# Weighting the fetched expert rows with a diagonal matrix on TensorE instead of scaling them on ScalarE and transposing

## The chip, the cores and the metric

One core of a Trainium2 chip runs the whole program. The metric is the device time of one execution in microseconds (us), the median of several runs. A profile is one more execution, taken by the hardware profiler.

## The reference

Two blocks of a language model on 256 tokens of width 1024, all in 32-bit floats. What matters here is the last part of each of the two layers of the second block, a feed-forward made of single experts. Each token picks 128 experts (8 heads x 16) of a table of 16384, by scores:

```python
expert = jnp.take_along_axis(cand_i, best_j, axis=-1)
gate = jax.nn.softmax(best_s, axis=-1)
act = jax.nn.gelu(jnp.einsum('btd,bthkd->bthk', xi, u_tab[expert]), approximate=False)
return jnp.einsum('bthk,bthkd->btd', (gate * act), v_tab[expert])
...
x = _layer_norm(DN_ALPHA * x + mix, ln1_g, ln1_b)
x = _layer_norm(DN_ALPHA * x + peer_ffn(x, peer_wq, peer_keys, peer_u, peer_v), ln2_g, ln2_b)
```

Every token needs 128 rows u (1024 wide) and 128 rows v (1024 wide) of its own; the result is the sum of the v rows, each times one number of that token and expert.

## The kernel before

The 256 tokens of a layer are two tiles of 128, so the second block has four tiles in order, i = 0 to 3 (layer i // 2, tokens i % 2). A tile has 128 **expert steps**, n = 128 i + k for k = 0 to 127, 512 in all. One step handles, for each of the 128 tokens (one for each partition), that token's k-th expert:

1. GpSimd (`fetch`, L2164 to L2171) issues an indirect DMA that brings 128 rows of 2048 floats (u and v side by side, 1.05 MB) from the table `in_puv` into `GR[n % PING]`. PING is 6, so the fetch of step n waits until TensorE is through with step n - 6 (`EP[n - PING]`).
2. VectorE (L2186) multiplies the u half by the token's row x and sums it into one number per partition.
3. ScalarE takes the Gelu of it (L2155), multiplies it by the gate (L2157) and then scales the v half, 1024 wide, by this number (L2160).
4. TensorE (L2141 to L2144) adds the scaled v half to PSUM banks 6 and 7 by eight transposes of 128 x 128, which accumulate over the 128 steps. So the sum stands there transposed.

When a tile's 128 steps are done, its closing part `fin` follows: VectorE (L2199) and ScalarE (L2263) copy banks 6 and 7 to the tile `YT`, TensorE transposes them back (`turn`, a helper at L435), VectorE adds them to x (L2205) and normalizes (L2209 to L2225), with one power on GpSimd (L2238). The first step of the next tile waits on TensorE until x has been added (`PV[i - 1, "x1"]`), since both use banks 6 and 7.

Between the expert steps of tile i stands the other work of tile i + 1 (the **lane**): projections (`fm` L1350, `tm` L1398), attention branches (`nsa` L1756 to L1785, `core` L1461 to L1509), gates (L1712), mixing (`mix`: L1888 and L1904), the `query` (L2017) and `route` (L2038 on TensorE, then sorting on VectorE) that pick the experts. The order is one written list, `plan`: every entry ("e", n) is one expert step, every entry (s, i) is one step of stream s of tile i. Each engine walks through the same list and issues its own part of each entry, in order; VectorE is at step n when ScalarE is at n - 1 and TensorE at n - 2. The lane of tile i + 1 is spread over the 128 entries by weights; the last tile has no lane but the closing part and its own routing. SyncE loads the weights of the lane in pieces of 1 MB into a ring of five slots, each load waiting until the slot's last reader on TensorE is through; these loads and the fetches share the same DMA engines.

Of the kernel before, what the change touches and what calls it, by code (L numbers as in the profile page):

```python
# [78 lines left out]
def build(nc, A, out):  # L79
# [4 lines left out]
    with ctx:  # L84
# [131 lines left out]
        SW2 = at(place(928), 928)  # L216
        scr = place(5554)
        GR = [at(place(2048), 2048) for i in range(PING)]
        YT = at(place(1024), 8, 128)
        IX = [at(place(128), 128).bitcast(u32) for t in range(2)]  # L220
        GT_ = [at(place(128), 128) for t in range(2)]
        DO = [at(place(128), 128) for t in range(2)]
# [39 lines left out]
                 + weave([("route", 20, 1), ("gates", 20, 1)])]  # L262
        for i in RI:
            placed_at = [(128.0 * i + k, ("e", 128 * i + k)) for k in range(128)]
            placed_at += [(128.0 * i + 1.1 + 0.1 * k, ("fin", i - 1)) for k in range(4) if i >= 1]
            lane = [("fin", i - 1)] * 8 * (i >= 1) + [(s, i + 1) for s in (tile_steps(i + 1) if i < 3 else [])]
            total, done = sum(weight[s] for s, _ in lane), 0.0
            for s in lane:
                placed_at.append((128.0 * i + 1.5 + 118 * done / total if i < 3 else 128.0 * i + 1.5 + done, s))
                done += weight[s[0]]  # L270
            lane = []
            for c in R3:
                lane += [("query", i)] * 8 + [("route", i)] * 20
            for n, s in enumerate(lane):
                placed_at.append((128.0 * i + 0.2 + 33.0 * n / len(lane), s))
            plan += [s for _, s in sorted(placed_at, key=lambda x: x[0])]
        plan += [("e", NE), ("e", NE + 1)] + [("fin", 3)] * 12


        RING2, SLOT2 = 5, 2048  # L280
# [2 lines left out]
                    tm=[("t", 0, 0, 3)] + [("t", n, 2 * n + 2, (7, 7, 11, 11, 13)[n - 1]) for n in range(1, 6)],  # L283
                    nsa=[("cw", 0, 0, 1)], gates=[("g", n, 2 * n, 4 * (n // 2) + 3) for n in range(16)],
                    mix=[("b", n, 2 * n + 2, 2 * n + 3) for n in R4] + [("o", n, 12 + n, 12 + (n | 1)) for n in R4] + [("ga", 0, 19, 21)],
                    query=[("q", n, 4 * n, 8 * (n // 2) + 7) for n in R8], fin=[("gf", 0, 8, 9)])
        step, nth2, last2 = {}, {}, {}
        for at_, s in enumerate(plan):
            n = step[s] = step.get(s, -1) + 1
# [115 lines left out]
        TA = marks("t_a", [(i, c, x) for i in RI for c in R4 for x in ("s", "e")])  # L405
        TV = marks("t_v", [(i, c, x) for i in RI for c in R4 for x in ("ix", "g3", "gt")])
        EP, EA, EV = [marks(n, range(NE)) for n in ("e_p", "e_a", "e_v")]
        PP = marks("p_p", [x for i in RI for x in [(i, "y0"), (i, "y1")] + [(i, c) for c in R2 if i < 2]])
        PV = marks("p_v", [(i, x) for i in RI for x in ["y", "x0", "x1", "st", "l"] + ["h"] * (i < 2)])
        PA = marks("p_a", [x for i in RI for x in [(i, "y")] + [(i, "h")] * (i < 2)])  # L410
        PO = marks("p_o", RI)


# [920 lines left out]
        def fm_pe(pe, i):  # L1334
            t = i % 2
            if i < 2:
                pe.wait_ge(*KV[t, 0])
                pe.wait_ge(*KA[t, 4])
            else:
                pe.wait_ge(*PV[i - 2, "h"])  # L1340
                pe.wait_ge(*PA[i - 2, "h"])
            for n in range(7):
                W = slot2(("f", i, n), 8, 256)
                pe.wait_ge(*landed2("f", i, n))
                if n in (4, 6):
                    pe.wait_ge(*MA[i, ("f", n // 2 - 2)])
                for h in R2:
                    o = bank(n // 2 % 2)[:, (n % 2 * 2 + h) * 128:(n % 2 * 2 + h) * 128 + 128]
                    for k in R8:
                        m = pe.matmul(o, W[:, k, h * 128:h * 128 + 128], HT[:, k, tsl(t)], start=k == 0, stop=k == 7)  # L1350
                        if k == 7 and h == 1 and (n % 2 == 1 or n == 6):
                            m.then_inc(MP.next((i, ("f", n // 2))), 1)
                        if k % 4 == 3:
                            yield
# [778 lines left out]
        def expert_pe(pe):  # L2133
            yield
            yield
            for n in range(NE):
                i, k = n // 128, n % 128
                if k == 0 and i:
                    pe.wait_ge(*PV[i - 1, "x1"])
                pe.wait_ge(*EA[n])  # L2140
                for c in R8:  # L2141
                    m = pe.matmul(bank(6 + c // 4)[:, tsl(c % 4)], GR[n % PING][:, 1024 + c * 128:1152 + c * 128], ident, is_transpose=True,  # L2142
                                  start=k == 0 and c % 4 == 0, stop=k == 127, skip_group_check=True)
                m.then_inc(EP.next(n), 1)  # L2144
                yield

        def expert_ac(ac):
            yield
            for n in range(NE):
                i, k = n // 128, n % 128  # L2150
                co, g = CO[i % 2][:, k:k + 1], GT_[i % 2][:, k:k + 1]
                if k % 32 == 0:
                    ac.wait_ge(*TV[i, k // 32, "gt"])
                ac.wait_ge(*EV[n])
                ac.activation(co, DO[i % 2][:, k:k + 1], ACT.Gelu).then_inc(oa.up(), 1)  # L2155
                ac.wait_ge(*oa.now())
                ac.activation(co, co, ACT.Copy, scale=g).then_inc(oa.up(), 1)  # L2157
                ac.wait_ge(*oa.now())
                v = GR[n % PING][:, 1024:2048]
                ac.activation(v, v, ACT.Copy, scale=co).then_inc(EA.next(n), 1)  # L2160
                yield
            yield

# [29 lines left out]
        def fin_ve(ve, i):  # L2193
            t = i % 2
            gb = slot2(("gf", i, 0), 2048)
            st, mv, v = ln_parts(t)
            x = X[:, t, :]
            ve.wait_ge(*EP[128 * i + 127])
            ve.tensor_copy(YT[:, 0:4, :], by(bank(6), 128)).then_inc(PV.next((i, "y")), 1)  # L2199
            yield  # L2200
            yield
            for h in R2:
                xx = x[:, h * 512:h * 512 + 512]
                ve.wait_ge(*PP[i, f"y{h}"])
                ve.scalar_tensor_tensor(xx, xx, al, bank(6 + h), MUL, ADD).then_inc(PV.next((i, f"x{h}")), 1)  # L2205
                yield
            ve.wait_ge(*PV[i, "x1"])
            for k in R2:
                ve.bn_stats(st[:, k * 6:k * 6 + 6], x[:, k * 512:k * 512 + 512]).then_inc(ov.up(), 1)  # L2209
            yield  # L2210
            ve.wait_ge(*ov.now())
            ve.bn_aggr(mv, by(st, 6)).then_inc(ov.up(), 1)
            yield
            ve.wait_ge(*ov.now())
            ve.tensor_scalar(v, v, 1.0, 1e-5, MUL, ADD).then_inc(PV.next((i, "st")), 1)
            yield
            ve.wait_ge(*PO[i])
            ve.tensor_scalar(x, x, mv[:, 0:1], v, SUB, MUL).then_inc(ov.up(), 1)
            yield
            ve.wait_ge(*landed2("gf", i, 0))  # L2220
            ve.wait_ge(*ov.now())
            ve.tensor_tensor(x, x, gb[:, 0:1024], MUL).then_inc(ov.up(), 1)
            yield
            ve.wait_ge(*ov.now())
            ve.tensor_tensor(x, x, gb[:, 1024:2048], ADD).then_inc(PV.next((i, "l")), 1)  # L2225
            yield
            yield
            if i < 2:
                ve.wait_ge(*PP[i, 0])
                ve.tensor_copy(HT[:, 0:4, tsl(t)], by(bank(0), 128)).then_inc(PV.next((i, "h")), 1)  # L2230
            yield

        def fin_po(po, i):
            v = ln_parts(i % 2)[2]
            for _ in R6:
                yield
            po.wait_ge(*PV[i, "st"])
            po.tensor_tensor(v, v, halfc, ALU.pow).then_inc(PO.next(i), 1)  # L2238
            for _ in R6:
                yield  # L2240

        def fin_pe(pe, i):
            yield
            for c in R2:
                pe.wait_ge(*(PV[i, "y"] if c == 0 else PA[i, "y"]))
                for k in R4:
                    m = turn(pe, bank(6 + c)[:, tsl(k)], YT[:, 4 * c + k, :])
                m.then_inc(PP.next((i, f"y{c}")), 1)
            yield
            for _ in R8:  # L2250
                yield
            if i < 2:
                pe.wait_ge(*PV[i, "l"])
                for c in R2:
                    for k in R4:
                        m = turn(pe, bank(c)[:, tsl(k)], X[:, i % 2, tsl(4 * c + k)])
                    m.then_inc(PP.next((i, c)), 1)
            yield
            yield

        def fin_ac(ac, i):
            ac.wait_ge(*EP[128 * i + 127])
            ac.activation(YT[:, 4:8, :], by(bank(7), 128), ACT.Copy).then_inc(PA.next((i, "y")), 1)  # L2263
            for _ in range(11):
                yield
            if i < 2:
                ac.wait_ge(*PP[i, 1])
                ac.activation(HT[:, 4:8, tsl(i % 2)], by(bank(1), 128), ACT.Copy).then_inc(PA.next((i, "h")), 1)
            yield


# [270 lines left out]
```

## Time and profile before

| | |
|---|---|
| time, median of 3 runs | 2911.42 us (2909.92 to 2918.89) |
| the profiled execution's own time | 2918.89 us |
| its span, first to last instruction | 2917.1 us |
| mean granted clock of TensorE | 0.869 of full speed |
| busy: TensorE, weight loads, VectorE, ScalarE, GpSimd | 81%, 69%, 48%, 45%, 25% of the span |
| expert steps: from the first transposes to the last | 1190 us to 2905 us |

"Granted clock" is the share of TensorE's full clock (2.4 GHz) that the chip let through, averaged over a stretch; at any moment it is one of two levels, 1.2 or 2.4 GHz. The DMA share is the mean busy share of the core's 16 DMA engines; it can read 1.01 by rounding. The expert steps fall into four **stages**, one for each tile, whose ends are the copies at L2199: at 1633, 2092, 2560 and 2905 us. A 32-bit matmul that is no transpose shows as two records, each with a weight load of its own; a transpose shows as one.

### The profile page before, as it was taken

The page shows a single profiled execution, that of the slowest core. Times are in us where ns is not written, and L with a number is a line of the kernel's source. Part 1 is how long each engine was busy: PE and PEld are TensorE (multiplying, and loading weights), DVE is VectorE, ACT ScalarE, POOL GpSimd, SP SyncE. Part 2 cuts the span into 40 slices and gives each one's busy share as a digit, 9 for nine tenths or more (in the row PEclk, how much of TensorE's full clock was granted, in tenths as well). Part 3 has the DMA queues.
Part 4 walks back from the last instruction along what each step waited for, and adds up shares of the span by engine and source line. Part 5 has one row for each costly group of instructions (what it writes and reads, how often), then busy time and mean ns, then how long its engine had stood idle before and what let it go on. Part 6 is the DMA issues. An engine that isn't in the chain of part 4 may idle for free.

```text
span 2917.1 us, 34012 instructions
## 1 busy us (share of the span) xinstructions
PE 2371.4 (81%) x13488; PEld 2003.1 (69%) x13488; DVE 1390.1 (48%) x3171; ACT 1310.5 (45%) x2339; POOL 737.8 (25%) x615
## 2 busy tenths in 40 slices
PE   7987998969999999878786788687698878666676
PEld 6766887856884878867665777566587766565554
DVE  3564333341001133474656764545765644676444
ACT  1551112110000220466755667764557674556665
POOL 0010112110000000232334323333322423334564
PEclk9988999989999999987777898899797988776666
DMA  6221111123433577998889999999998999999997
GB/s 257 87 89 58 59 65 58 51 101 126 163 144 139 218 271 288 395 420 347 306 348 422 403 421 383 409 408 415 396 420 355 407 366 420 401 380 351 421 421 318
DMA packets 109999, 839.34 MB, mean 288 GB/s; under 512 B 12176, under 2 KB 12432, under 8 KB 13968
## 3 DMA queue, kind: packets, MB, share of 16 engines
q0 software_dynamic: 73728, 536.90, 45.6%
q1 hardware_dynamic: 36112, 300.25, 26.2%
q8 instruction: 107, 1.75, 0.2%
q14 instruction: 52, 0.43, 0.0%
HBM read 836.06 MB, written 1.05 MB: 287 GB/s over the span
## 4 chain that ended last, share of the span: by engine, by line
PE 50%; DMA 20%; DVE 13%; ACT 12%; issue 3%; POOL 1%; SPq 0%; DVEq 0%; POOLq 0%; ACTq 0%
DMA mem<-in_puv,mem 19%; PE psm L431 10%; PE psm L2142 7%; PE psm L439 5%; PE psm L1712 5%; DVE mem L2186 4%; ACT mem L2160 4%; PE psm L718 3%; PE psm L2017 3%; PE psm L1247 3%; PE psm L1350 2%; PE psm L1904 2%; ACT L2155 1%; PE psm L733 1%; PE psm L435 1%
## 5 line engine op out<-in xcount | busy, mean ns | idle before, releaser
L2142 PE MATMUL psm<-mem 128*128 128x128 f32 x4096 | 706.6, 331 | 365.3 <-ACT mem L2160 364.7
L2142 PEld LDWEIGHTS psm<-mem 128*128 128x128 f32 x4096 | 587.4, 172 | 480.4 <-ACT mem L2160 464.8
L2170 POOL DMA_INDIRECT mem<-in_puv,mem x512 | 618.0, 1207 | 1111.0 <-PE psm L2142 1036.0
L2186 DVE CUSTOM_DVE_ANT_0 mem<-mem 128x1024 f32<-128x1024 f32 x512 | 624.5, 1225 | 436.2 <-DMA mem<-in_puv,mem 435.4
L2160 ACT ACTIVATE mem<-mem 128x1024 f32<-128x1024 f32 x512 | 588.8, 1150 | 16.7
L431 PE MATMUL psm<-mem 128*128 128x256 f32 (+2 forms) x1504 | 352.6, 398 | 32.6 <-DVE mem L1180 17.1
L431 PEld LDWEIGHTS psm<-mem 128*128 128x128 f32 x1504 | 293.2, 198 | 91.3 <-issue 29.5
L2155 ACT ACTIVATE mem<-mem 128x1 f32<-128x1 f32 x512 | 101.8, 199 | 457.2 <-DVE mem L2186 456.3
L1712 PE MATMUL psm<-mem 128*128 128x256 f32 x1024 | 245.4, 392 | 0.5 <-ACT mem L1426 0.5
L1712 PEld LDWEIGHTS psm<-mem 128*128 128x128 f32 x1024 | 195.9, 197 | 27.7 <-ACT mem L1426 0.9
L439 PEld LDWEIGHTS psm<-mem 128*128 128x128 f32 x1408 | 178.7, 192 | 45.2 <-issue 22.0
L439 PE MATMUL psm<-mem 128*128 128x128 f32 x1408 | 190.3, 279 | 19.4 <-ACT mem L986 5.9
L2157 ACT ACTIVATE mem<-mem 128x1 f32<-128x1 f32 x512 | 150.8, 294 | 16.6
L718 PE MATMUL psm<-mem 128*128 128x256 f32 x576 | 150.1, 384 | 0.0
L2017 PE MATMUL psm<-mem 128*128 128x128 f32 x1024 | 133.3, 286 | 6.3 <-DMA mem<-in_pwq 5.6
L2017 PEld LDWEIGHTS psm<-mem 128*128 128x128 f32 x1024 | 127.7, 202 | 8.6 <-DMA mem<-in_pwq 6.4
L986 ACT ACTIVATE mem<-psm 128x512 f32<-128x512 f32 x64 | 38.2, 597 | 209.8 <-PE psm L439 151.0
L1350 PE MATMUL psm<-mem 128*128 128x128 f32 x896 | 113.1, 279 | 7.9 <-DVE mem L2230 4.6
L435 PE MATMUL psm<-mem 128*128 128x128 f32 (+1 forms) x352 | 63.5, 319 | 62.4 <-DVE mem L1002 20.8
L1350 PEld LDWEIGHTS psm<-mem 128*128 128x128 f32 x896 | 107.2, 195 | 9.4 <-DVE mem L2230 5.2
L718 PEld LDWEIGHTS psm<-mem 128*128 128x128 f32 x576 | 100.3, 193 | 11.6 <-issue 3.9
L435 PEld LDWEIGHTS psm<-mem 128*128 128x128 f32 (+1 forms) x352 | 47.8, 162 | 76.3 <-DVE mem L1002 21.2
(357 smaller groups left out, 2435.5 us busy)
## 6 DMA issues: line engine op xcount, KB each, us to landing
mem<-in_w2g SPq DMA_DIRECT2D x64, 1024.0 KB, 8.9
mem<-in_w SPq DMA_DIRECT2D x18, 2048.0 KB, 8.3
mem<-in_pwq SPq DMA_DIRECT2D x32, 1024.0 KB, 11.5
mem<-in_w2f SPq DMA_DIRECT2D x28, 1024.0 KB, 10.1
mem<-in_wgu SPq DMA_DIRECT2D x11, 2048.0 KB, 7.9
mem<-in_w2t SPq DMA_DIRECT2D x20, 1024.0 KB, 11.9
mem<-in_w2b SPq DMA_DIRECT2D x16, 1024.0 KB, 10.7
mem<-in_w2o SPq DMA_DIRECT2D x16, 1024.0 KB, 9.6
```

What stands on the lines that cost most here:

```text
L431: m = pe.matmul(o, lhs(k), rhs(k), start=start and k == ks[0], stop=stop and k == ks[-1])
L435: return pe.transpose(o, i, ident[0:i.shape[0], 0:i.shape[0]])
L439: m = pe.matmul(b[:, u * 128:u * 128 + 128], lhs(u), rhs(u), start=True, stop=True)
L718: m = pe.matmul(o, W[:, k, c0:c0 + 128], HT[:, k, :], start=k == 0, stop=k == 7)
L1350: m = pe.matmul(o, W[:, k, h * 128:h * 128 + 128], HT[:, k, tsl(t)], start=k == 0, stop=k == 7)
L1712: m = pe.matmul(gates_bank(i, n // 2)[:, n % 2 * 256:n % 2 * 256 + 256], HT[:, k, tsl(t)], W[:, k, :], start=k == 0, stop=k == 7)
L2017: m = pe.matmul(o, W[:, k, h * 128:h * 128 + 128], HT[:, k, tsl(t)], start=k == 0, stop=k == 7)
L2142: m = pe.matmul(bank(6 + c // 4)[:, tsl(c % 4)], GR[n % PING][:, 1024 + c * 128:1152 + c * 128], ident, is_transpose=True, start=k == 0 an ...
L2157: ac.activation(co, co, ACT.Copy, scale=g).then_inc(oa.up(), 1)
L2160: ac.activation(v, v, ACT.Copy, scale=co).then_inc(EA.next(n), 1)
L2170: po.indirect_dma_start(GR[n % PING], None, A[f"puv{i // 2}"], bass.IndirectOffsetOnAxis(ap=IX[i % 2][:, k:k + 1], axis=0)).then_inc(gsem[ ...
L2186: ve.tensor_tensor_reduce(out=GR[n % PING][:, 0:1024], in0=GR[n % PING][:, 0:1024], in1=X[:, i % 2, :], scale=1.0, scalar=0.0, op0=MUL, op ...
```

## The change

ScalarE no longer scales the v half. It writes a 128 x 128 matrix with the token's number on the diagonal (the identity `ident` scaled per partition by `co`) into one of four buffers `DG`, and waits before it for the step that used the buffer four steps earlier. TensorE then multiplies this diagonal, as the stationary operand, with the v half as it was fetched, in two matmuls of 512 columns, accumulated in banks 6 and 7. The sum then stands in PSUM as tokens x features, so the two copies to `YT`, the eight transposes back and their waits go, and VectorE adds banks 6 and 7 to x at once. The first four steps of `fin`, which stood at 1.1 to 1.4 entries after the stage's start, and the eight others become ten in the lane, from 1.5 entries on; the steps after the addition move up by two. `YT` (1024 floats per partition) gives way to `DG` (512).

```diff
-        YT = at(place(1024), 8, 128)
+        DG = at(place(512), 4, 128)
...
-            placed_at += [(128.0 * i + 1.1 + 0.1 * k, ("fin", i - 1)) for k in range(4) if i >= 1]
-            lane = [("fin", i - 1)] * 8 * (i >= 1) + [(s, i + 1) for s in (tile_steps(i + 1) if i < 3 else [])]
+            lane = [("fin", i - 1)] * 10 * (i >= 1) + [(s, i + 1) for s in (tile_steps(i + 1) if i < 3 else [])]
...
-        plan += [("e", NE), ("e", NE + 1)] + [("fin", 3)] * 12
+        plan += [("e", NE), ("e", NE + 1)] + [("fin", 3)] * 10
...
-                for c in R8:
-                    m = pe.matmul(bank(6 + c // 4)[:, tsl(c % 4)], GR[n % PING][:, 1024 + c * 128:1152 + c * 128], ident, is_transpose=True,
-                                  start=k == 0 and c % 4 == 0, stop=k == 127, skip_group_check=True)
+                for h in R2:
+                    m = pe.matmul(bank(6 + h), DG[:, n % 4, :], GR[n % PING][:, 1024 + h * 512:1536 + h * 512], start=k == 0, stop=k == 127)
                 m.then_inc(EP.next(n), 1)
...
-                v = GR[n % PING][:, 1024:2048]
-                ac.activation(v, v, ACT.Copy, scale=co).then_inc(EA.next(n), 1)
+                if n >= 4:
+                    ac.wait_ge(*EP[n - 4])
+                ac.activation(DG[:, n % 4, :], ident, ACT.Copy, scale=co).then_inc(EA.next(n), 1)
...
             ve.wait_ge(*EP[128 * i + 127])
-            ve.tensor_copy(YT[:, 0:4, :], by(bank(6), 128)).then_inc(PV.next((i, "y")), 1)
-            yield
-            yield
             for h in R2:
                 xx = x[:, h * 512:h * 512 + 512]
-                ve.wait_ge(*PP[i, f"y{h}"])
                 ve.scalar_tensor_tensor(xx, xx, al, bank(6 + h), MUL, ADD).then_inc(PV.next((i, f"x{h}")), 1)
...
-            yield
-            for c in R2:
-                pe.wait_ge(*(PV[i, "y"] if c == 0 else PA[i, "y"]))
-                for k in R4:
-                    m = turn(pe, bank(6 + c)[:, tsl(k)], YT[:, 4 * c + k, :])
-                m.then_inc(PP.next((i, f"y{c}")), 1)
-            yield
...
-            ac.wait_ge(*EP[128 * i + 127])
-            ac.activation(YT[:, 4:8, :], by(bank(7), 128), ACT.Copy).then_inc(PA.next((i, "y")), 1)
-            for _ in range(11):
+            for _ in range(9):
```

## Rows read from the trace of the kernel before

**Rows 1.** The page, costliest groups: busy us, mean ns of one, idle before.

```profile
L2142 PE MATMUL psm<-mem 128*128 128x128 f32 x4096 | 706.6, 331 | 365.3 <-ACT mem L2160 364.7
...
L2160 ACT ACTIVATE mem<-mem 128x1024 f32<-128x1024 f32 x512 | 588.8, 1150 | 16.7
...
L2157 ACT ACTIVATE mem<-mem 128x1 f32<-128x1 f32 x512 | 150.8, 294 | 16.6
```

**Rows 2.** Windows by stage: length, busy PE PEld DVE ACT POOL, clock, DMA, GB/s.

```profile
1190.00:1633.00 443.00, 334.85 (x2059) 294.17 (x2059) 261.58 (x651) 277.94 (x487) 153.70 (x133) 0.79 0.94 372
1633.00:2092.00 459.00, 351.60 (x2287) 304.76 (x2285) 263.30 (x662) 283.08 (x500) 155.19 (x135) 0.88 0.99 405
2092.00:2560.00 468.00, 372.41 (x2358) 324.13 (x2356) 271.52 (x665) 284.29 (x500) 157.17 (x135) 0.86 0.97 396
2560.00:2905.00 345.00, 239.95 (x1227) 198.85 (x1225) 202.93 (x459) 219.63 (x397) 171.90 (x124) 0.66 0.96 389
```

**Rows 3.** Windows of the transposes L2142 alone, the same stages (PE, PEld, clock, DMA).

```profile
1190.00:1633.00 443.00, 174.10 (x1019) 146.71 (x1020) 0.79 0.94 372
1633.00:2092.00 459.00, 155.76 (x1031) 130.54 (x1029) 0.88 0.99 405
2092.00:2560.00 468.00, 160.19 (x1026) 135.78 (x1024) 0.86 0.97 396
2560.00:2905.00 345.00, 216.46 (x1027) 174.34 (x1025) 0.66 0.96 389
```

**Rows 4.** Timeline near 2747 us, last stage: two steps' transposes, a fetch between.

```profile
2746.37 1.83 PE L2142 MATMUL psm<-mem 128*128 128x128 f32 x8 [0.58 <-ACT mem L2160]
...
2748.47 1.82 POOL L2170 DMA_INDIRECT mem<-in_puv,mem  x1 [0.66 <-PE psm L2142]
...
2748.80 1.10 PE L2142 MATMUL psm<-mem 128*128 128x128 f32 x8 [0.60 <-ACT mem L2160]
```

**Rows 5.** Timeline of TensorE, back to back: transposes and 512-column matmuls in turn.

```profile
1483.65 1.88 PE L1888 MATMUL psm<-mem 128*128 128x512 f32 x4
1485.37 1.04 PE L2142 MATMUL psm<-mem 128*128 128x128 f32 x8
1486.25 1.88 PE L1888 MATMUL psm<-mem 128*128 128x512 f32 x4
```

**Rows 6.** The chain near 1994 us: a burst of 256-column matmuls after transposes alone.

```profile
1994.09 3.41 PE psm L1904 x8
...
1998.38 3.46 PE psm L1904 x16
```

**Rows 7.** Groups by form: ScalarE over 128 x 128 with one operand for each partition.

```profile
L1801 ACT ACTIVATE mem<-mem 128x128 f32<-128x128 f32 x16 | 6.3, 393 | 2.9 <-DVE mem L1843 2.9
```

**Rows 8.** Windows of three shorter stretches, columns as in rows 2.

```profile
1314.00:1533.00 219.00, 169.93 (x936) 144.10 (x937) 114.95 (x239) 143.72 (x248) 74.27 (x64) 0.74 0.87 334
2117.00:2190.00 73.00, 66.91 (x547) 63.25 (x545) 45.57 (x139) 42.59 (x76) 20.85 (x20) 0.98 1.01 420
2190.00:2263.00 73.00, 61.81 (x390) 54.77 (x391) 41.06 (x117) 49.88 (x82) 19.59 (x18) 0.79 0.85 345
```

**Rows 9.** Windows of the transposes L2142 alone, the same stretches (PE, clock, DMA).

```profile
1314.00:1533.00 219.00, 84.54 (x480) 0.74 0.87 334
2117.00:2190.00 73.00, 20.86 (x152) 0.98 1.01 420
2190.00:2263.00 73.00, 22.26 (x144) 0.79 0.85 345
```

**Rows 10.** The chain, by line, within 1314 to 1533 us, then 2190 to 2263 us.

```profile
by line: DMA mem<-in_puv,mem 15.4%; PE psm L2142 14.8%; ACT mem L2160 10.0%; PE psm L1904 6.1%; ACT L2155 4.1%; DVE mem L2186 3.8%; PE psm L1758 3.2%; PE psm L1756 3.0%; ACT mem L2157 2.5%; issue 2.5%; PE psm L1888 2.4%; ACT mem L1801 2.0%;
...
by line: PE psm L2142 14.8%; ACT mem L2160 14.2%; PE psm L1712 9.6%; PE psm L1758 9.5%; ACT L2155 8.8%; ACT L1529 7.0%; PE psm L1398 6.2%; PE psm L1756 5.3%; PE psm L1469 4.5%; ACT mem L2157 3.8%; issue 3.0%; ACT mem L2155 2.0%; ACT mem L15
```

**Rows 11.** Timeline of the end: the last transposes, then the addition.

```profile
2903.12 1.96 PE L2142 MATMUL psm<-mem 128*128 128x128 f32 x8 [0.47 <-ACT mem L2160]
...
2906.56 1.28 DVE L2205 SCALAR_TENSOR_TENSOR mem<-mem,psm 128x512 f32<-128x512 f32 x2 [0.76 <-PE psm L435]
```

More of the change, by code:

```diff
@@ L285, in build @@
                     mix=[("b", n, 2 * n + 2, 2 * n + 3) for n in R4] + [("o", n, 12 + n, 12 + (n | 1)) for n in R4] + [("ga", 0, 19, 21)],
-                    query=[("q", n, 4 * n, 8 * (n // 2) + 7) for n in R8], fin=[("gf", 0, 8, 9)])
+                    query=[("q", n, 4 * n, 8 * (n // 2) + 7) for n in R8], fin=[("gf", 0, 6, 7)])
         step, nth2, last2 = {}, {}, {}
@@ L407, in build @@
         EP, EA, EV = [marks(n, range(NE)) for n in ("e_p", "e_a", "e_v")]
-        PP = marks("p_p", [x for i in RI for x in [(i, "y0"), (i, "y1")] + [(i, c) for c in R2 if i < 2]])
-        PV = marks("p_v", [(i, x) for i in RI for x in ["y", "x0", "x1", "st", "l"] + ["h"] * (i < 2)])
-        PA = marks("p_a", [x for i in RI for x in [(i, "y")] + [(i, "h")] * (i < 2)])
+        PP = marks("p_p", [(i, c) for i in R2 for c in R2])
+        PV = marks("p_v", [(i, x) for i in RI for x in ["x0", "x1", "st", "l"] + ["h"] * (i < 2)])
+        PA = marks("p_a", R2)
         PO = marks("p_o", RI)
@@ L1340, in fm_pe @@
                 pe.wait_ge(*PV[i - 2, "h"])
-                pe.wait_ge(*PA[i - 2, "h"])
+                pe.wait_ge(*PA[i - 2])
             for n in range(7):
@@ L2234, in fin_po @@
             v = ln_parts(i % 2)[2]
-            for _ in R6:
+            for _ in range(4):
                 yield
@@ L2267, in fin_ac @@
                 ac.wait_ge(*PP[i, 1])
-                ac.activation(HT[:, 4:8, tsl(i % 2)], by(bank(1), 128), ACT.Copy).then_inc(PA.next((i, "h")), 1)
+                ac.activation(HT[:, 4:8, tsl(i % 2)], by(bank(1), 128), ACT.Copy).then_inc(PA.next(i), 1)
             yield
```

## The prediction

> **What bounds the kernel now.** I read the windows by stage first. In the four stages of expert steps the DMA engines are busy 0.94, 0.99, 0.97 and 0.96 of the time [rows 2]. The reader is to see that no engine comes near that: TensorE 76, 77, 80 and 70%, ScalarE 63, 62, 61 and 64%. A stretch with a DMA share of 1.01 moves 420 GB/s [rows 8]; I take this as the ceiling. A fetch of 1.05 MB is then 2.5 us, and 128 of them 320 us, to which the lane's weights are added. All idle DMA time in the stages is 0.06 x 443 + 0.01 x 459 + 0.03 x 468 + 0.04 x 345 = 27 + 5 + 14 + 14 = 60 us. The change moves no byte, so what it can give is at most these 60 us and the end of the kernel.
>
> The same windows in shorter stretches show where the idle DMA time lies: 28 us from 1314 to 1533 us (share 0.87 of 219 us) and 11 us from 2190 to 2263 us (0.85 of 73 us) [rows 8]. These are the attention parts of the lane, where work goes back and forth between the engines. The chain says what the time goes by there: it passes through transposes, ScalarE's scaling and the table changes of the Gelu (L2155 without "mem"), with the fetches only 15% of the first stretch and none of the second's leading lines [rows 10].
>
> The page's groups give the price of the two operations to be replaced: 1150 ns for the scaling, and 706.6 us in all for 4096 transposes, 1.38 us for a step's eight [rows 1]. This is a mean over two clocks. In the timeline eight transposes last 1.10 us or 1.83 us within two and a half us of each other [rows 4], and the granted clock of the last stage, where TensorE does little else, is 0.66, that of the mixed stages 0.79 to 0.88 [rows 2].
>
> **The change part by part.**
>
> *ScalarE.* 512 times 1150 ns over 1024 columns becomes 128 columns. The nearest row is an activation of that shape with one operand for each partition, 393 ns [rows 7]. That saves 0.757 us a step, 97 us of ScalarE a stage, leaving it near 40% busy. The new wait for the step four earlier is priced at nothing: TensorE has ended step n - 4 two fetches after step n - 6, which lets fetch n begin, and fetch n has yet to arrive. If that cover fails, what waits behind it on ScalarE are its lane activations, and TensorE is late anyway then.
>
> *TensorE.* Eight transposes become two matmuls of 512 columns, four records. Between 1483.65 and 1486.25 us both kinds stand back to back at full clock: four records of 512 columns take 1.72 us, eight transposes 0.88 us [rows 5]. So a step costs 1.72 us at full clock, 0.84 us more than the transposes at full clock, and about as much as they do at the low one.
>
> What that makes of the clock decides the sum. After waiting with only transposes before it, a burst of eight records of 256 columns took 3.41 us (0.43 us each, the low clock); right after it sixteen took 3.46 us (0.22 us each, the high one) [rows 6]. Ordinary matmuls brought the clock up within one burst. The new step is such a burst in every 2.5 us, so I take the clock as full through all stages. The Trainium skill says in "TensorE: Matmul & The Clock Gate", Part 4, that transposes do not count towards the fast clock the way matmuls do; the 0.66 of the last stage, with TensorE 70% busy, agrees.
>
> TensorE's work by stage is then its other work at full clock plus 128 x 1.72 = 220 us. The other work is the difference of busy times times the granted clock [rows 2, 3]:
> - stage 0: (334.85 - 174.10) x 0.79 = 127; with 220, 347 us, 78% of 443
> - stage 1: (351.60 - 155.76) x 0.88 = 172; 392 us, 86% of 459 (77% before)
> - stage 2: (372.41 - 160.19) x 0.86 = 183; 403 us, 86% of 468 (80% before)
> - stage 3: (239.95 - 216.46) x 0.66 = 16; 236 us, 68% of 345.
>
> It stays below the DMA engines' time in each, though not in each stretch. From 2117 to 2190 us it was 66.91 us busy (92%) beside a full DMA [rows 8]; so 92% still leaves the DMA full. There it becomes (66.91 - 20.86) x 0.98 + 19 x 1.72 = 77.8 us in 73 [rows 8, 9]: 5 us longer. This is the front of a stage: `fm` beside `query` and `route`. Stage 1 has the same front, 5 us, and I give stage 0 half, 2 us. Loss: 12 us.
>
> *The slack stretches.* From 1314 to 1533 us the scaling is 10.0% of the chain, 21.9 us, and shrinks by 0.757 / 1.15: -14.4 us. Transposes are 14.8%, 32.4 us; a step's cost there 84.54 / 60 = 1.41 us [rows 9], so 23 steps pay 0.31 us more: +7.1 us. The small matmuls L1756 and L1758, 13.6 us of the chain, speed up from a clock of 0.74 to 1, about -3.5 us. Sum -10.8 us, of 28 to be had. From 2190 to 2263 us likewise: scaling 14.2%, 10.4 us, -6.8; transposes 10.8 us at 22.26 / 18 = 1.24 us a step, 8.7 steps, +4.2; other matmuls 35% of the chain, 25.6 us, at 0.79, -5.4. Sum -8.0 us, of 11. For the 20 us of idle DMA left elsewhere I take a quarter, -5 us, because much of it lies near sorting on VectorE, which stays.
>
> *The closing part.* The last transposes start at 2903.12 us and the addition at 2906.56 us, 3.44 us later [rows 11]. After, the last step starts 0.76 us earlier, its four records last 1.88 us from first start to last end [rows 5], and the addition follows at once: -2.3 us. In the three stages before, the copies and transposes go as well, but VectorE now does an expert step between the two halves of the addition, because its two steps stand half an entry apart. I set this against each other: nothing. On GpSimd the power waits for VectorE's variance with the fetches queued behind it; it moves up by the same two steps as that variance, so the wait keeps its length. The lane behind the closing part shifts by about one entry of 128, and its loads with it: nothing. If that cover is gone it costs one step of 2.5 us a stage.
>
> **The sum.** -10.8 - 8.0 - 5 - 2.3 + 12 = -14 us. Against the profiled execution's own 2918.9 us this is 2905 us. That execution was the slowest of the three, 7.5 us above the median, so I forecast 2897 us beside the median of 2911.4.
>
> Bounds: the diagonal lies between 294 ns, the price of one column [rows 1], and 1150 ns, that of 1024, but far nearer to the row of its own shape; at 294 ns the two chains above give 3 us more, at 1150 ns they give back the 21 us won on ScalarE. The slack can give 60 us at most, and nothing at least. The dense fronts can cost from nothing (buffers absorb it: six fetches and five weight slots) to 25 us.
>
> **The rivals.**
>
> *TensorE becomes the bound of the mixed stages.* 86% is an average the engine has not had here, since the lane's matmuls come in bursts and wait for other engines. It decides where TensorE can't be held above some share: at 82% busy, stage 1 takes 392 / 0.82 = 478 us (+19) and stage 2 403 / 0.82 = 491 us (+23). With -11 us from stage 0 and -2 us at the end this is +29 us, 2940 us. At 86% it costs nothing, at 80% +69 us less 13. For it: the 77 to 80% of before. Against it: 92% in one stretch with a full DMA, and that TensorE's largest wait in before, 364.7 us for the scaling [rows 1], is time that it can fill.
>
> *The DMA hides everything.* What the slack stretches give back, the dense fronts take, and only the end is left: -2 us, 2909 us. For it: shares of 0.96 and more in three stages.
>
> *More of the slack is used.* If ScalarE's 97 us a stage is what keeps fetches waiting all over, half of the 60 us comes back and the fronts cost little: about -35 us, 2876 us. Against it: the fetches are on most of the chain where the DMA is full, and there ScalarE's time buys nothing.
>
> *The clock stays low.* A step would cost 3.41 us, as the eight records of 256 columns did [rows 6], and the last stage 128 x 3.41 + 23 = 460 us in place of 345: 3025 us, more if the mixed stages follow. Against it: rows 6.
>
> *The matmul costs four transposes' time.* A step is then 4 x 0.88 = 3.5 us at full clock, over a fetch's 2.5: the stages become 572, 617, 628 and 461 us, 563 us more, 3475 us. That is what the Trainium skill would make of it, in "TensorE: Matmul & The Clock Gate", Terms: the transpose mode is four times as fast for 32-bit data. The rows show 1.72 against 0.88 us, a factor of 2.0, for the same 1024 columns.
>
> **How the numbers follow.** The exchange as summed, 2880 to 2914 us: 0.42. More of the slack, 2855 to 2880: 0.10. DMA hides everything: 0.15. TensorE the bound, 2920 to 2965: 0.28. Clock low 0.04, four times 0.01. A measurement here tells 0.3% from no change, 2902.7 to 2920.2 us. Of the first case about three quarters lies below that, all of the second; of the others, the third is inside and the rest above: faster 0.44, no change 0.25, slower 0.31. The range leaves out the low clock, the four times and the ends of two cases: 2865 to 2950 us.
>
> **What would show it.** In the profile after: L2142 as 2048 records of 512 columns, four in 1.72 us; L2160 near 0.39 us; a granted clock of 0.95 or more in all stages; no L2199, L2263; the addition right behind the last step. The stretch 1314 to 1533 us shorter with a fuller DMA, the fronts of stages 1 and 2 longer with TensorE above 92%. Wrong would be: stages 1 and 2 longer than 459 and 468 us with a DMA share below 0.93 and TensorE in full use, or a stage 3 unlike 345 us.

## The result and the profile after

The changed kernel takes 2941.78 us, median of 4 runs (2937.18 to 2946.53; three more executions took 2939.60, 2946.96 and 2948.82 us), against 2910.67 us for the kernel before (4 runs): a ratio of 1.0108, 95% interval 1.0085 to 1.0133. It is 31 us slower, where 2897 us was forecast. The profiled execution has a span of 2942.0 us and a mean granted clock of 0.959, against 0.869.

Lines have moved: L2142 is now L2141, L2160 is L2159, L2170 is L2169, L435 is L434. First the page of the changed kernel, its costliest groups:

```profile
L2141 PE MATMUL psm<-mem 128*128 128x512 f32 x2048 | 1017.6, 626 | 157.9 <-ACT mem L2159 153.2
...
L2159 ACT ACTIVATE mem<-mem 128x128 f32<-128x128 f32 x512 | 206.0, 402 | 16.9
```

Against [rows 1], ScalarE's 588.8 us are 206.0 us, as priced (402 ns against 393 ns). The steps' matmuls are busy 1017.6 us in place of 706.6 us, and TensorE's idle time before them, most of it waiting for ScalarE, fell from 365.3 to 157.9 us.

Then the windows of the four stages, all engines, and the step's matmuls alone (columns as in [rows 2, 3]; the stages end at the additions, at 1625, 2103, 2581 and 2932 us):

```profile
1190.00:1625.00 435.00, 390.72 (x1553) 227.84 (x1552) 261.67 (x652) 185.23 (x488) 148.47 (x133) 0.95 0.95 379
1625.00:2103.00 478.00, 435.35 (x1759) 271.25 (x1758) 262.52 (x661) 185.27 (x500) 153.59 (x135) 0.95 0.96 390
2103.00:2581.00 478.00, 443.92 (x1837) 280.07 (x1836) 270.18 (x664) 186.48 (x495) 149.69 (x135) 0.96 0.95 384
2581.00:2932.00 351.00, 277.87 (x705) 112.11 (x703) 202.74 (x459) 124.85 (x396) 127.90 (x124) 0.98 0.96 385
```

```profile
1625.00:2103.00 478.00, 252.18 (x512) 94.19 (x512) 0.95 0.96 390
2103.00:2581.00 478.00, 250.90 (x513) 94.24 (x512) 0.96 0.95 384
```

Stages 1 and 2 lasted 459 and 468 us, now 478 and 478. TensorE is busy 91 and 93% in them (77 and 80% before), the granted clock is 0.95 and more, and the DMA share fell from 0.99 and 0.97 to 0.96 and 0.95: no more bytes, but more time in which the DMA engines had nothing to move. ScalarE went from 62 to 39%.

TensorE's own waits in stages 1 and 2 say where the idle time went. Before, from 1633 to 2560 us (waiter, who was waited for, us in total, times, longest):

```profile
PE psm L2142 <- ACT mem L2160: 165.9, 96, 7.4
...
PE psm L435 <- DVE mem L2225: 5.1, 2, 2.6
```

and after, from 1625 to 2581 us:

```profile
PE psm L2141 <- ACT mem L2159: 46.5, 38, 5.0
PE psm L434 <- DVE mem L2220: 13.3, 2, 6.6
```

The wait for the step's input shrank by 119 us, and all of TensorE's idle time in the two stages by 126 us, from 203 to 77 us. Its busy time grew by 435.35 + 443.92 - 351.60 - 372.41 = 155 us. The difference, 29 us, is what the two stages got longer. This is bookkeeping and names no cause yet.

### The profile page after: what moved, and what is told of

The parts are those of the page before. It is cut to its first block, busy times and chain, and to the rows that moved or that the text cites. A ratio compares the mean times of both kernels' runs of the same rounds, so it can differ in the third digit from the quotient of the medians.

```text
span 2942.0 us, 30348 instructions
## 1 busy us (share of the span) xinstructions
PE 2618.3 (89%) x11408; PEld 1770.9 (60%) x11408; DVE 1387.1 (47%) x3167; ACT 925.3 (31%) x2331; POOL 679.5 (23%) x615
## 4 chain that ended last, share of the span: by engine, by line
PE 62%; DMA 15%; DVE 12%; ACT 8%; issue 2%; POOL 1%; SPq 0%; DVEq 0%; POOLq 0%; ACTq 0%
PE psm L2141 16%; DMA mem<-in_puv,mem 13%; PE psm L430 10%; PE psm L1711 6%; PE psm L438 5%; DVE mem L2185 3%; PE psm L717 3%; PE psm L2016 3%; PE psm L1349 3%; PE psm L1246 3%; PE psm L1903 2%; PE psm L1397 1%; DMA mem<-in_pwq 1%; PE psm L434 1%; PE psm L732 1%
## 5 line engine op out<-in xcount | busy, mean ns | idle before, releaser
L2141 PE MATMUL psm<-mem 128*128 128x512 f32 x2048 | 1017.6, 626 | 157.9 <-ACT mem L2159 153.2
L2169 POOL DMA_INDIRECT mem<-in_puv,mem x512 | 563.0, 1100 | 1209.6 <-PE psm L2141 1141.6
L2141 PEld LDWEIGHTS psm<-mem 128*128 128x128 f32 x2048 | 373.7, 196 | 609.1 <-ACT mem L2159 300.4
L430 PEld LDWEIGHTS psm<-mem 128*128 128x128 f32 x1504 | 291.2, 196 | 92.0 <-issue 32.1
L1711 PEld LDWEIGHTS psm<-mem 128*128 128x128 f32 x1024 | 197.2, 194 | 56.7 <-issue 31.4
L2159 ACT ACTIVATE mem<-mem 128x128 f32<-128x128 f32 x512 | 206.0, 402 | 16.9
L438 PE MATMUL psm<-mem 128*128 128x128 f32 x1408 | 190.3, 279 | 19.4 <-ACT mem L985 5.9
L438 PEld LDWEIGHTS psm<-mem 128*128 128x128 f32 x1408 | 178.7, 192 | 45.3 <-issue 22.0
L2016 PEld LDWEIGHTS psm<-mem 128*128 128x128 f32 x1024 | 125.8, 195 | 29.8 <-issue 22.2
L2016 PE MATMUL psm<-mem 128*128 128x128 f32 x1024 | 128.8, 279 | 5.8 <-DMA mem<-in_pwq 5.1
L1349 PEld LDWEIGHTS psm<-mem 128*128 128x128 f32 x896 | 108.5, 192 | 22.5 <-issue 21.3
L434 PE MATMUL psm<-mem 128*128 128x128 f32 (+1 forms) x320 | 53.9, 304 | 67.8 <-DVE mem L1001 20.8
L1349 PE MATMUL psm<-mem 128*128 128x128 f32 x896 | 110.3, 275 | 2.0 <-DMA mem<-in_w2f 1.2
L717 PEld LDWEIGHTS psm<-mem 128*128 128x128 f32 x576 | 100.1, 193 | 11.3 <-issue 3.6
L434 PEld LDWEIGHTS psm<-mem 128*128 128x128 f32 (+1 forms) x320 | 41.2, 154 | 97.6 <-issue 32.7
## 6 DMA issues: line engine op xcount, KB each, us to landing
mem<-in_pwq SPq DMA_DIRECT2D x32, 1024.0 KB, 10.8
```

The source lines that it names most:

```text
L430: m = pe.matmul(o, lhs(k), rhs(k), start=start and k == ks[0], stop=stop and k == ks[-1])
L434: return pe.transpose(o, i, ident[0:i.shape[0], 0:i.shape[0]])
L438: m = pe.matmul(b[:, u * 128:u * 128 + 128], lhs(u), rhs(u), start=True, stop=True)
L717: m = pe.matmul(o, W[:, k, c0:c0 + 128], HT[:, k, :], start=k == 0, stop=k == 7)
L1711: m = pe.matmul(gates_bank(i, n // 2)[:, n % 2 * 256:n % 2 * 256 + 256], HT[:, k, tsl(t)], W[:, k, :], start=k == 0, stop=k == 7)
L2141: m = pe.matmul(bank(6 + h), DG[:, n % 4, :], GR[n % PING][:, 1024 + h * 512:1536 + h * 512], start=k == 0, stop=k == 127)
```

## The experiments

The step numbers n let two profiles be laid on each other. The table has the time from VectorE's start on step a to that on step b, from the timeline's rows of its product (L2186 of the kernel before), in us. Each is one execution.

| kernel | 0 to 128 | 128 to 256 | 256 to 384 | 384 to 511 | 128 to 144 | 160 to 176 | 288 to 304 |
|---|---|---|---|---|---|---|---|
| before | 457.0 | 459.3 | 468.5 | 343.6 | 61.6 | 60.8 | 65.9 |
| before, again | 450.7 | 461.4 | 465.3 | 345.2 | 59.2 | 62.3 | 63.3 |
| changed | 449.5 | 477.5 | 479.2 | 349.4 | 73.2 | 68.3 | 71.8 |
| changed, again | 449.2 | 476.3 | 480.3 | 348.5 | 71.6 | 68.3 | 70.0 |
| scalar_only | 444.5 | 456.4 | 457.9 | 341.4 | 60.6 | 57.8 | 61.7 |
| tensor_only | 458.7 | 481.6 | 491.4 | 350.1 | 70.2 | 72.0 | 72.9 |
| half_columns | 451.3 | 456.0 | 459.6 | 343.4 | 62.6 | 62.7 | 64.4 |
| three_quarters | 444.8 | 465.3 | 470.6 | 346.3 | 67.4 | 64.4 | 66.2 |
| closing_early | 447.3 | 473.1 | 482.0 | 348.3 | 65.8 | 64.8 | 67.0 |
| front_thinned | 456.0 | 475.4 | 486.7 | 346.5 | 63.5 | 66.3 | 68.5 |

**Two more profiles: before_again, after_again.** Both kernels unchanged, one execution each. Expected:

> The kernel before once more, for a second profile. It says how far the start of a given expert step moves between two executions of one kernel; theory A's reading of the stages needs this to be within some 5 us at step 384, while a first profile that was slow by itself in stage 0 would take away the changed kernel's lead of 7.5 us at step 128.

> The changed kernel once more, for a second profile with the same aim. Theory A: steps 128 to 144 and 256 to 272 take 70 to 73 us again, against 60 to 62 us in the kernel before.

Measured: 2914.36 and 2942.84 us. The changed kernel repeats within 2 us in every column. The kernel before repeats within 3.2 us but for stage 0, where the first profile was 6 us slow. So most of the lead of 7.5 us that the changed kernel seemed to have at step 128 was that of one execution: against the second profile it is 3 us at step 128, 1.5 us over the stage. The losses in stages 1 and 2 (15 to 18 and 11 to 15 us) and in stage 3 (3 to 6 us) stand.

**ScalarE's part alone: scalar_only.**

```diff
-                v = GR[n % PING][:, 1024:2048]
+                v = GR[n % PING][:, 1024:1152]
```

> The kernel before, with ScalarE scaling only the first 128 of a v half's 1024 columns; the other 896 go into the sum unscaled. It has ScalarE's relief (1150 to about 400 ns a step) and nothing of TensorE's part. Theory A, TensorE's longer step is what costs the time and ScalarE's relief wins some: 10 to 25 us below the kernel before, about 2893 us. Theory B, the DMA hides ScalarE's relief altogether: 2911 us within 4.

Measured: 2891.21 us, ratio 0.9929 (0.9908 to 0.9949), 21 us faster. Its windows by stage (all engines):

```profile
1190.00:1618.00 428.00, 325.07 (x2049) 286.42 (x2049) 259.72 (x648) 183.83 (x484) 153.79 (x133) 0.80 0.96 383
1618.00:2075.00 457.00, 356.98 (x2284) 312.73 (x2283) 264.42 (x663) 189.23 (x500) 156.00 (x136) 0.87 0.99 408
2075.00:2532.00 457.00, 360.88 (x2361) 316.47 (x2360) 271.12 (x667) 191.74 (x500) 153.60 (x135) 0.88 0.98 403
```

With ScalarE as idle as in the changed kernel, TensorE is at 76 to 79% and the DMA share is 0.96 to 0.99. The relief reaches the end, a little in every stage.

**TensorE's part alone: tensor_only.**

```diff
-                    m = pe.matmul(bank(6 + h), DG[:, n % 4, :], GR[n % PING][:, 1024 + h * 512:1536 + h * 512], ...)
+                    m = pe.matmul(bank(6 + h), ident, GR[n % PING][:, 1024 + h * 512:1536 + h * 512], ...)
...
-                if n >= 4:
-                    ac.wait_ge(*EP[n - 4])
-                ac.activation(DG[:, n % 4, :], ident, ACT.Copy, scale=co).then_inc(EA.next(n), 1)
+                v = GR[n % PING][:, 1024:2048]
+                ac.activation(v, v, ACT.Copy, scale=co).then_inc(EA.next(n), 1)
```

> The changed kernel, with ScalarE scaling the whole v half as before and TensorE multiplying by the plain identity in two matmuls of 512 columns. It has TensorE's part and the new closing part, and nothing of ScalarE's relief. Theory A, TensorE's longer step costs and ScalarE's relief wins: above the changed kernel's 2942 us by what ScalarE wins, 2950 to 2970 us. Theory B, the diagonal's own wait for the step four earlier holds ScalarE up: no slower than the changed kernel, 2942 us or less, since that wait is gone.

Measured: 2978.4 us, ratio 1.0227 (1.0204 to 1.0249), 65 us slower and 8 us beyond what was expected. The four kernels make a square, each beside the kernel before:

| | transposes | two matmuls of 512 columns, new closing part |
|---|---|---|
| ScalarE scales 1024 columns | 1 | 1.0227 |
| ScalarE's short operation | 0.9929 | 1.0108 |

TensorE's part costs 2.3% by itself and 1.8% (1.0108 / 0.9929) beside the relief; the relief is worth 0.7% beside transposes and 1.2% (1.0108 / 1.0227) beside the matmuls. The wait for the step four earlier isn't the cause. The slower tensor_only, which lacks it, also lacks the relief and so can't tell alone; but in the page of the changed kernel ScalarE is idle before the diagonal for 16.9 us in all 512 steps, against 16.7 us before the scaling [rows 1].

**A dose of TensorE's time: half_columns and three_quarters.** The same step with 256 or 384 of 512 columns in each matmul.

```diff
-                for h in R2:
-                    m = pe.matmul(bank(6 + h), DG[:, n % 4, :], GR[n % PING][:, 1024 + h * 512:1536 + h * 512], start=k == 0, stop=k == 127)
+                w = 512 if k in (0, 127) else 256
+                for h in R2:
+                    m = pe.matmul(bank(6 + h)[:, 0:w], DG[:, n % 4, :], GR[n % PING][:, 1024 + h * 512:1024 + h * 512 + w], start=k == 0, stop=k == 127)
```

> The changed kernel, with each matmul of a step over 256 columns in place of 512, but for the first and last step of a tile; the second half of each bank lacks 126 of 128 steps. A step costs TensorE 0.86 us, as the transposes did at full clock; ScalarE, the closing part and the clock stay as changed. Theory A, TensorE's time is the cause: the whole loss goes and ScalarE's gain is left, 2875 to 2900 us. Theory C, the closing part or the order of the plan is the cause: 2930 us or more.

> The changed kernel, with each matmul of a step over 384 columns in place of 512, but for the first and last step of a tile; a quarter of each bank lacks 126 of 128 steps. A step costs TensorE 1.29 us at full clock. 256 columns gave 2896 us, 512 give 2942 us. Theory A, TensorE's time adds up along the stretches where TensorE is the bound: about halfway, 2912 to 2925 us. Theory D, the loss comes from the clock's rise or from reading 512 columns at once: near one of the two ends.

Measured: 2896.32 us with 256 columns, ratio 0.9940 (0.9918 to 0.9961); 2915.84 us with 384, ratio 1.0012 (0.9997 to 1.0026); 1.0108 with 512. Everything but the width is the changed kernel (part of the sum is left out), so its loss goes with TensorE's time. By the ratios the first step of 128 columns adds 21 us and the second 28 us, of 512 x 0.43 = 220 us at full clock each (an estimate: a step's four records, each 128 columns or 0.11 us longer): a tenth of it, then an eighth, reaches the end. One expectation was missed: the clock did not stay as changed. With half the columns it fell to 0.872 (0.945 with 384); so the first of these steps mixes width and clock.

**The closing part: closing_early.** The addition's two halves back at entries 1.1 and 1.2.

```diff
+            placed_at += [(128.0 * i + 1.1 + 0.1 * k, ("fin", i - 1)) for k in range(2) if i >= 1]
-            lane = [("fin", i - 1)] * 10 * (i >= 1) + ...
+            lane = [("fin", i - 1)] * 8 * (i >= 1) + ...
```

> The changed kernel, with the two halves of the closing addition put back ahead of the next tile's second expert step (entries 1.1 and 1.2), the other eight closing steps as in the kernel before. Theory A, TensorE's longer step is the cause: it wins back little, 2935 to 2942 us. Theory C, the closing part's new place is the cause, since TensorE waits 6.6 us for the normalized x at the front of stages 1 and 2, 2.6 us before: it wins back 10 us or more, 2932 us or less.

Measured: 2937.51 us, ratio 1.0087 (1.0065 to 1.0109), beside 1.0108 (1.0085 to 1.0133). The two intervals overlap. At the front of stage 1 the steps 128 to 144 do get shorter, 65.8 us against 73.2 and 71.6, and TensorE's wait for the normalized x, 13.3 us above, is 4.4 us in its trace:

```profile
PE psm L435 <- DVE mem L2221: 4.4, 2, 2.2
```

but most isn't kept to the end: stages 1 and 2 together (steps 128 to 384) take 955.1 us, against 956.7 and 956.6 us. By the medians it is 4 to 6 us of the 31, and the intervals don't tell it from nothing.

**The order of the plan: front_thinned.** The same kernel, with the lane less dense at a stage's front:

```diff
-                placed_at.append((128.0 * i + 1.5 + 118 * done / total if i < 3 else 128.0 * i + 1.5 + done, s))
+                placed_at.append((128.0 * i + 1.5 + 118 * (done / total) ** 0.85 if i < 3 else 128.0 * i + 1.5 + done, s))
```

> The kernel with the closing part early again (2937.5 us), and the lane's steps spread less densely at the front of a stage: the share of the lane done is raised to the power 0.85 to give its place among the entries. No work is changed. Theory A says that TensorE is the bound in the dense fronts and nearly everywhere in stages 1 and 2 (91% busy), so the front gets shorter and the rest longer: 2925 to 2940 us. If the density of the fronts alone is the cause, 2915 us or less.

Measured: 2955.1 us, ratio 1.0142 (1.0115 to 1.0169): slower than either expected. The front did get shorter (128 to 144 in 63.5 us) and the rest lost more: against closing_early, stage 0 is 9 us longer, stage 1 2 us and stage 2 5 us. That an even spread doesn't help agrees with a TensorE that is short of time nearly everywhere, but why it costs some 16 us (by the ratios) was not traced, and stage 0, the largest loss, is not one where the changed kernel loses.

**Where TensorE has room: tile_0 and tiles_0_3.** The kernel before, with the changed step for some tiles only (`DIAG = (0,)` or `(0, 3)`, `if i in DIAG` at each changed place).

> The kernel before, with the diagonal and the two matmuls for the steps of tile 0 alone; tiles 1 to 3 keep scaling and transposes. Up to step 128 the changed kernel was 7.5 us ahead, in the stage whose lane is lightest. Theory A: 4 to 10 us below the kernel before, about 2906 us, since TensorE is not the bound in stage 0. If the steps cost alike everywhere, a quarter of the loss: 2919 us.

> The kernel before, with the diagonal and the two matmuls for tiles 0 and 3, which have the lightest lanes, and the closing part of these two in its short form, early. Theory A: the gain of tile 0 and the 2 us of the shorter end, against some 4 us at the front of stage 3 with its query and route: 2900 to 2910 us.

Measured: 2910.8 us, ratio 0.9996 (0.9983 to 1.0009), and 2911.64 us, ratio 0.9994 (0.9981 to 1.0008). Neither gains or loses. Both expectations leaned on the first profile of the kernel before, slow in stage 0, and fell with it. In stage 0 of tile_0 (window of all engines) the step's price is paid and refunded. Its first 16 steps take 75.1 us (71.1 and 69.6 in the two profiles of the kernel before), its steps 36 to 96 212.9 us (224.0 and 216.8):

```profile
1190.00:1625.00 435.00, 388.61 (x1577) 228.74 (x1576) 263.41 (x656) 187.46 (x490) 149.76 (x135) 0.96 0.95 380
```

**The relief without TensorE's price: vector_half.** The kernel before, with VectorE scaling half of the columns one step behind its product:

```diff
-                v = GR[n % PING][:, 1024:2048]
+                v = GR[n % PING][:, 1024:1536]
...
+                if n:
+                    scale_half(ve, n - 1)
...
+        def scale_half(ve, n):
+            v = GR[n % PING][:, 1536:2048]
+            ve.wait_ge(*EA[n])
+            ve.tensor_scalar(v, v, CO[n // 128 % 2][:, n % 128:n % 128 + 1], None, MUL).then_inc(EW.next(n), 1)
```

> The kernel before, with the scaling of the v half shared: ScalarE scales 512 columns and VectorE, one step behind its own product, the other 512; transposes and closing part stay. ScalarE's relief without TensorE's longer step. With only 128 columns scaled on ScalarE, and nowhere else, the time was 2891 us. Theory A: ScalarE is on the path where the DMA is slack; 0.43 of the 0.75 us a step gives some 12 us, less what VectorE's added 0.45 us costs in the sorting stretches: 2898 to 2908 us. If VectorE's in-order wait for ScalarE holds its lane up: 2915 us or more.

Measured: 2967.29 us, ratio 1.0166 (1.0141 to 1.0192), as the other branch of the expectation had it, only more. VectorE's waits:

```profile
DVE mem L2198 <- ACT mem L2160: 151.0, 75, 15.1
```

VectorE, the engine that starts every step, now stands 151 us behind ScalarE, with its lane and its next product behind that wait. That this wait makes the loss is argued, not tested. No version tried beats the kernel before with its work whole.

## Why the prediction was wrong

**What held.** The step's price and form, back to back in the changed kernel at full clock (timeline of TensorE), 1.72 us a step as [rows 5] said:

```profile
2129.12 1.89 PE L2141 MATMUL psm<-mem 128*128 128x512 f32 x4
2130.84 1.95 PE L1349 MATMUL psm<-mem 128*128 128x128 f32 x16
2132.63 1.89 PE L2141 MATMUL psm<-mem 128*128 128x512 f32 x4
```

The factor of 2 against transposes held, so the rival with a factor of 4 fell, and so did the one of a low clock: 0.95 to 0.98 by stage, though full "through all stages", as forecast, it was not. The end, in the timeline of the changed kernel:

```profile
2929.49 1.99 PE L2141 MATMUL psm<-mem 128*128 128x512 f32 x4 [0.47 <-ACT mem L2159]
2931.51 1.28 DVE L2200 SCALAR_TENSOR_TENSOR mem<-mem,psm 128x512 f32<-128x512 f32 x2 [3.08 <-PE psm L2141]
```

From the last step's first record to the addition it is 2.02 us, and 3.44 us in [rows 11]; with the 0.75 us that ScalarE is faster, -2.2 us against -2.3 forecast.

**The step that failed** is what was drawn from the sentence that TensorE's work "stays below the DMA engines' time in each, though not in each stretch", with 86% of stages 1 and 2: that the DMA engines' time would cover it, but for 12 us in the dense fronts, and that the slack stretches would gain 10.8 and 8.0 us. The work measured, 435 and 444 us, is 95% of the 459 and 468 us before; it is still below the DMA engines' time, and it wasn't covered. Three things were wrong.

1. *The work was too small.* It had 392 and 403 us for stages 1 and 2; busy are 435 and 444 us. The step's matmuls are busy 252 and 251 us where 220 were counted. A step lasts 1.89 us from first start to last end also back to back (0.17 us of it beside the next records) and 1.99 us alone, as at 2929.49 above; and 8 steps of stage 1 and 7 of stage 2 met the low clock and took 2.3 to 3.8 us. The other work is 183 and 193 us where 172 and 183 were counted. Times the granted clock of 0.95 and 0.96 it is 174 and 185 us: this other work was counted right, and the clock that was taken as full is not full, above all at the small attention matmuls (last section).

2. *The fronts.* Forecast was 5 us each in stages 1 and 2. Steps 128 to 144 took 10 to 14 us more and with closing_early 4 to 7 us more. So the term was about right for TensorE's work, and the other half came from the closing part, costed at nothing. The timeline of the changed kernel at the front of stage 1 shows how:

```profile
1628.67 2.82 PE L2141 MATMUL psm<-mem 128*128 128x512 f32 x4 [2.06 <-DVE mem L2200]
...
1635.03 0.60 ACT L2027 ACTIVATE mem<-psm 128x512 f32<-128x512 f32 x1 [9.24 <-PE psm L2016]
...
1638.33 0.87 DVE L2059 MAX8 mem<-mem 128x8 f32<-128x128 f32 x4 [6.96 <-ACT mem L2048]
...
1640.26 0.81 DVE L2213 TENSOR_SCALAR mem<-mem 128x1024 f32<-128x1024 f32 x1
...
1647.84 1.97 PE L434 MATMUL psm<-mem 128*128 128x128 f32 x8 [6.64 <-DVE mem L2220]
```

TensorE first waits 2.06 us for the second half of the addition, which stands behind an expert step on VectorE. Its query matmuls (L2016) come later by that and partly at the low clock, ScalarE and VectorE wait for them (the sorting at L2059), and the normalization (L2213 to L2220) stands behind the sorting in VectorE's order. So TensorE waits 6.6 us for x in place of 2.6 us. In closing_early two of the normalization's three passes stand ahead of the sorting, and TensorE's wait is 2.2 us. As most of that is lost again later in the stage, the closing part explains half of the front's loss and little of the 31 us.

3. *The attention stretches.* This is the sign error. There the DMA had slack, and I took from it that ScalarE's relief would fill it, with TensorE's longer steps only on the part of the chain that they held. But in such a stretch of the kernel before (1754 to 1815 us, steps 160 to 176), TensorE's wait for ScalarE was short:

```profile
PE psm L2142 <- ACT mem L2160: 6.7, 4, 4.5
```

6.7 us in 61 us is all that a faster ScalarE could shorten or a longer TensorE could fill (scalar_only takes 3.0 to 4.5 us off these steps). After, the wait is 0.2 us and TensorE fills its windows (1760 to 1828 us, 2232 to 2303.5 us, all engines):

```profile
1760.00:1828.00 68.00, 65.17 (x294) 42.51 (x293) 27.78 (x73) 32.16 (x76) 19.95 (x18) 0.87 0.82 327
2232.00:2303.50 71.50, 67.28 (x309) 45.30 (x307) 29.78 (x74) 33.27 (x78) 19.56 (x18) 0.88 0.78 314
```

Busy 96 and 94%, with DMA shares of 0.82 and 0.78: so what the DMA lacked was fetches released by TensorE, and its slack grew: GpSimd's fetches wait 48 us for TensorE in the first of these windows, and 36 us in the stretch of the kernel before. These 16 steps take 6 to 8 us and 4 to 9 us longer, where 8 us less were forecast for the stretch of the second. The low clock adds to it: at 2279.94 us a step takes 3.73 us, and the eight transposes in its place took 1.97 us (last section), so there the exchange costs 1.8 us and not 0.84 us.

Of the gain of 10.8 us from 1314 to 1533 us a part came. Steps 36 to 96 took 224.0 us in the profile it was read from and 216.8 us in the second; in the changed kernel they take 212.1 and 213.9 us. That is 3 to 5 us against the second profile. The front of stage 0 took it back, priced at 2 us: steps 0 to 16 take 74.7 and 74.6 us, against 71.1 and 69.6 us. The stage as a whole gives 1 to 2 us (steps 0 to 128: 450.7 us before, 449.5 and 449.2 us after).

**The rival that came true** is "TensorE becomes the bound of the mixed stages": 2940 us, by stages of 478 and 491 us at 82%. Measured were 2941.8 us, 478 and 478 us; the forecast work over the measured length is 392 / 478 = 82% and 403 / 478 = 84%. It got the sum largely by luck. Its condition, that TensorE can't be held above 82%, did not hold: TensorE was busy 91 and 93%, and the 82% comes out only because the forecast work was too small by as much. It also took 11 us from stage 0, which gave 1 to 2 us, 23 us for stage 2, which lost 11 to 15, and nothing for stage 3, which lost 3 to 6. What is right in it is that TensorE became the bound. The argument used against it, that TensorE's largest wait "is time that it can fill", is what the runs settle. In stages 1 and 2 it filled 119 of 166 us, and the rest of the added work came on top. Half_columns and three_quarters show that TensorE's time makes the loss, and the square shows that ScalarE's relief is real and worth less. Why a tenth to an eighth of the added time reaches the end, and not more or less, is argued from the waits and was not measured on its own.

Two slips in the prediction's sums change nothing here. By its own cases, slower comes to 0.33 and faster to 0.42, where it has 0.31 and 0.44; and at 80% busy the two stages take 67 us more, where it has 69.

## What to carry to other kernels

When work moves from one engine to another, weigh what the receiving engine waits for in each stretch, not its busy share over a stage: the new work is free only up to that wait. A slack DMA beside an engine that hardly waits is a sign that this engine is the bound, also when the chain of waits names others. Take a second profile before a difference of some microseconds between two stretches carries an argument.

## What the hardware showed that was not expected

**Low clock with ordinary matmuls too.** The prediction laid the low clock of the last stage to transposes, with the Trainium skill's rule in "TensorE: Matmul & The Clock Gate", Part 4, that they don't count towards the fast clock as matmuls do. The runs don't show a difference of kind. In the last stage of half_columns, where each step is four records of ordinary matmuls, 200 us have a granted clock of 0.64, in the changed kernel 1.00, and in the kernel before 0.63 (half_columns: window and a step in the timeline; then the windows of the changed kernel and of the kernel before):

```profile
2700.00:2900.00 200.00, 140.45 (x303) 79.47 (x301) 98.07 (x159) 67.45 (x225) 68.89 (x71) 0.64 0.93 385
...
2799.55 2.07 PE L2142 MATMUL psm<-mem 128*128 128x256 f32 x4 [0.41 <-ACT mem L2160]
```

```profile
2700.00:2900.00 200.00, 159.42 (x324) 55.03 (x323) 96.34 (x157) 70.50 (x235) 80.13 (x82) 1.00 1.01 420
...
2700.00:2900.00 200.00, 141.10 (x640) 113.26 (x640) 98.82 (x160) 131.61 (x241) 115.93 (x77) 0.63 1.00 417
```

The 640 records before are all transposes, so a mean of 0.63 says that with transposes alone the full clock was granted for about a quarter of the time. half_columns and the changed kernel differ in the columns of a step alone. The kind of matmul doesn't explain the low clock here.

**The clock falls under the small attention matmuls.** In `nsa` TensorE works through 64 records over 64 partitions with 15 columns each, then 64 with 64 columns each (with 7 for 15 in stage 1), without a gap between them. In the kernel before (timeline, then windows of the two bursts):

```profile
2239.01 3.93 PE L1756 MATMUL psm<-mem 64*64 64x15 f32 x64
2242.87 7.00 PE L1758 MATMUL psm<-mem 64*15 64x64 f32 x64
2249.80 1.97 PE L2142 MATMUL psm<-mem 128*128 128x128 f32 x8
...
2239.00:2242.87 3.87, 3.87 (x65) 3.83 (x65) 1.23 (x2) 2.86 (x5) 0.95 (x1) 0.98 1.00 417
2242.87:2249.87 7.00, 7.00 (x66) 6.80 (x66) 0.00 (x0) 0.13 (x1) 0.00 (x0) 0.50 0.81 338
```

and in the changed kernel:

```profile
2265.03 4.58 PE L1755 MATMUL psm<-mem 64*64 64x15 f32 x64
2269.54 7.00 PE L1757 MATMUL psm<-mem 64*15 64x64 f32 x64
...
2279.94 3.73 PE L2141 MATMUL psm<-mem 128*128 128x512 f32 x4
...
2269.54:2276.54 7.00, 7.00 (x66) 6.80 (x65) 0.00 (x0) 0.00 (x0) 0.00 (x0) 0.50 0.32 132
```

The clock is 0.98 under the first burst of the kernel before and 0.50 under the second in both, and what follows still meets the low level. This repeats at each of the three places in all 13 profiles: under the second burst the granted clock is 0.50 to 0.65. The small matmuls do take their time from the clock: the same first burst lasts 3.9 us at 1.00 and 6.97 us at 0.50 (1350.44 us in before_again). So TensorE can be busy without a gap and fall to the low clock, and the step's new matmuls around these bursts didn't keep it up. What in the small matmuls brings it down was not tested.
